# A hybrid attention, SSD and mixture-of-experts layer: VectorE's work of the attention stage in another order, Silu of z later, and ended groups' values copied out of PSUM by ScalarE

## The reference

```python
s = einsum(q, k_cmp) - slopes * dist;  p_cmp = masked_softmax(s);  o_cmp = p_cmp @ v_cmp   # 63 compressed keys
imp = p_cmp @ ov;  idx = top_k(score(imp), 8)                                              # blocks of 64 keys
o_slc = softmax over the chosen blocks @ v_sel                                             # up to (c+1)*128 keys
o_win = softmax over the last 256 keys @ v_win                                             # up to 384 keys
o = gate0 * o_cmp + gate1 * o_slc + gate2 * o_win
# SSD: chunks of 128 tokens; y = (C B^T * decay) X + C state * decay; the output is y * silu(z)
```

## Time and profile before

| | us |
|---|---|
| median of three runs | 1086.52 |
| lowest, highest | 1084.16, 1087.3 |
| the profiled execution | 1083.51 |
| its span | 1081.8 |
| TensorE busy | 1017.3 (94%) |
| VectorE busy | 645.0 (60%) |
| ScalarE busy | 323.3 (30%) |
| GpSimd busy | 175.2 (16%) |

### The profile page before, as it was taken

How to read it: one execution, slowest core, us unless ns; L and a number is a source line. 1 busy time by engine, 2 the same in 40 slices (tenths; PEclk the granted TensorE clock), 3 DMA queues, 4 the chain that set the end, 5 groups by cost and what they waited for, 6 DMA issues and landing times.

```text
span 1081.8 us, 14029 instructions
## 1 busy us (share of the span) xinstructions
PE 1017.3 (94%) x4628; PEld 609.3 (56%) x4629; DVE 645.0 (60%) x1629; ACT 323.3 (30%) x766; POOL 175.2 (16%) x214
## 2 busy tenths in 40 slices
PE   5999999999999899999999899999949999999995
PEld 3444475444556677777788785555524444444442
DVE  2431121555354678666632798765578787878883
ACT  3321121112133566555656564232211000000000
POOL 0020051111000400000000400211021333333432
PEclk9999999999999899999999899999969999999998
DMA  7311042013000200000000503323649879998331
GB/s 256 100 32 40 1 81 78 1 39 101 1 1 1 79 2 1 1 1 1 2 1 1 195 2 103 126 86 110 233 151 374 286 243 333 373 367 308 126 107 70
DMA packets 73686, 119.21 MB, mean 110 GB/s; under 512 B 14016, under 2 KB 53152, under 8 KB 73632
## 3 DMA queue, kind: packets, MB, share of 16 engines
q1 hardware_dynamic: 62544, 87.55, 23.9%
q0 software_dynamic: 11088, 30.95, 8.1%
HBM read 105.37 MB, written 21.50 MB: 117 GB/s over the span
## 4 chain that ended last, share of the span: by engine, by line
PE 52%; DVE 14%; issue 2%; ACT 2%; POOL 0%; DVEq 0%; POOLq 0%; ACTq 0%
PE ps L1763 16%; PE ps L1116 8%; PE ps L1773 8%; PE ps L2086 5%; PE ps L1084 4%; PE ps L1095 4%; DVE ring_gate_up L1246 2%; PE ps L2096 2%; PE ps L1137 2%; DVE misc L285 2%; PE ps L2117 1%; DVE big_u L2302 1%; ACT big_u L1192 1%; DVE ring_down L2424 1%; DVE big_u L1533 1%
## 5 line engine op out<-in xcount | busy, mean ns | idle before, releaser
L1577 DVE STREAM_TRANSPOSE big_w<-big_w 32x256 f32<-32x256 f32 x384 | 167.3, 436 | 30.6 <-DMA big_w<-hn_dram,misc 24.4
L1763 PE MATMUL ps<-ring_gate_up,big_w 128*128 (+1 forms) x400 | 180.6, 595 | 0.0
L498 PE MATMUL ps<-big_w,big_u 128*128 128x512 f32 (+1 forms) x448 | 173.4, 542 | 0.0
L498 PEld LDWEIGHTS ps<-big_w,big_u 128*128 128x128 f32 x448 | 83.8, 191 | 76.0 <-issue 69.3
L1116 PEld LDWEIGHTS ps<-ring_down,big_u 128*128 128x128 f32 x912 | 112.3, 196 | 23.6 <-issue 12.1
L1116 PE MATMUL ps<-ring_down,big_u 128*128 128x65 f32 x912 | 118.6, 277 | 7.3 <-DVEq L1271 3.7
L1763 PEld LDWEIGHTS ps<-ring_gate_up,big_w 128*128 128x128 f32 x400 | 74.5, 192 | 83.8 <-issue 83.8
L1246 DVE CUSTOM_DVE_ANT_0 ring_gate_up<-ps,ring_down 128x384 f32<-128x384 f32 (+7 forms) x128 | 73.8, 629 | 64.8 <-PE ps L1084 63.7
L1192 ACT ACTIVATE big_u<-ps 128x512 f32<-128x512 f32 (+1 forms) x126 | 69.5, 582 | 125.1 <-PE ps L1095 125.0
L1184 ACT ACTIVATE ring_gate_up<-ring_gate_up,big_w 128x64 f32<-128x64 f32 (+8 forms) x192 | 92.2, 555 | 1.1 <-DVE big_w L1246 1.1
L1773 PE MATMUL ps<-ring_down,big_w 128*128 x200 | 90.0, 593 | 0.6 <-ACT big_w L1807 0.6
(11 more groups left out here) (384 smaller groups left out, 1325.4 us busy)
## 6 DMA issues: line engine op xcount, KB each, us to landing
ring_gate_up<-in_w_gate SPq DMA_DIRECT2D x16, 1024.0 KB, 10.0
ring_gate_up<-in_w_up SPq DMA_DIRECT2D x16, 1024.0 KB, 12.7
ring_down<-in_w_down SPq DMA_DIRECT2D x16, 1024.0 KB, 14.8
misc<-in_x SPq DMA_DIRECT2D x16, 512.0 KB, 3.4
big_w<-in_w_in SPq DMA_DIRECT2D x6, 1024.0 KB, 7.7
big_w<-in_w_out SPq DMA_DIRECT2D x8, 512.0 KB, 4.9
hn_dram<-big_u SPq DMA_DIRECT2D x8, 512.0 KB, 2.6
out<-ring_gate_up SPq DMA_DIRECT2D x8, 512.0 KB, 3.8
```

Source lines behind the costliest of these rows:

```text
L498: last = nc.tensor.matmul(ps[:, b, 0:width], uT[:, k, c * P:(c + 1) * P], wbuf[:, n % 2, k, 0:width], start=(k == 0), stop=(k == KD - 1))
L1577: last = nc.vector.transpose(dst[j * 32:(j + 1) * 32, :, i * 32:(i + 1) * 32], src[i * 32:(i + 1) * 32, :, j * 32:(j + 1) * 32])
L1763: last = nc.tensor.matmul(ps[:, 2 + b, :], xT[:, b, k, :], ring_gu[:, bass.ds(at + k * 2 * D_EXP, BANK)], start=(k == 0), stop=(k == KD - 1))
```

## The change

1. ScalarE gets `copy_values(gi)`: one Copy of both value banks (128 x 520 float32, 648 for CMP) into SBUF (`o_copy`), for each group but the last, after `exponentials(j)` of iteration j = last slot + 2. `o_read` now counts these copies; VectorE's reads of the copy are counted by `o_used`, for which the next copy waits.
2. `read_values` reads `o_copy` (for the last group still PSUM) and waits for the copy.
3. In VectorE's iteration, `read_values` stands ahead of `select` and `queries`, and the quarters of the queries start at the CMP slot of a chunk, not at its WIN slot.
4. z's pieces fill six slots, not seven, and the wait for the copies stands ahead of the second pair of slot 7's scores.
5. Silu of z and the table load move behind the decay exponentials of SSD chunk 0; VectorE's product with z waits for it at chunk 3 (`z_ready`).
6. `chunk_in(0)` (now a function of its own, called by `first_vector`, its operations the same) runs on VectorE ahead of the last `read_values`. TensorE's state product of chunk 0 waits for the attention rows (`rows_done`).
7. `weightsT` takes other places in the same buffer, so that the SSD operands of chunk 0 don't lie on it.

```diff
@@ -943,7 +943,8 @@
     q_rows = M["q_rows"]
     scores_full, max_ready, exp_done = sem("scores_full"), sem("maxima_ready"), sem("exp_done")
     wT_full, wT_done = sem("weights_transposed"), sem("weightsT_copied")
-    pv_done, o_read = sem("slot_values_done"), sem("values_read")
+    pv_done, o_read, o_used = sem("slot_values_done"), sem("values_copied"), sem("copied_values_used")
+    o_copy = M["misc"][:, 2048:2048 + NG * GQ * (HD + 17)].rearrange("p (g n) -> p g n", g=NG)
     sel_ready, sel_full, sel_rows = sem("selection_ready"), sem("selection_transposed"), sem("selection_rows")
...
@@ -999,7 +1000,8 @@
 
     def weightsT(j, k):
 
-        return uT[:, 4 * ((J - 1 - j) % 2) + k, 0:BANK]
+        at = ((4096, 6144, 4608, 6656) if (J - 1 - j) % 2 == 0 else (0, 1024, 2048, 3072))[k]
+        return M["big_u"][:, at:at + BANK]
 
     heads_before, copies_before = [0], [0]
...
@@ -1024,19 +1026,19 @@
 
     queries_at = {0: [(1, 0), (1, 1)], 1: [(1, 2), (1, 3)]}
     for c in range(1, NT - 1):
-        j0, n = first_slot[WIN, c], first_slot[CMP, c + 1] - first_slot[WIN, c]
+        j0, n = first_slot[CMP, c], first_slot[CMP, c + 1] - first_slot[CMP, c]
         for quarter in range(4):
             queries_at.setdefault(j0 + quarter * n // 4, []).append((c + 1, quarter))
 
     first_wide = first_slot[WIN, 2]
     n_pieces = (NT - Z_HEAD) * KD
     piece_at, done = {}, 0
-    for j in range(first_wide):
-        n = n_pieces * (j + 1) // first_wide - done
+    for j in range(first_wide - 1):
+        n = n_pieces * (j + 1) // (first_wide - 1) - done
         piece_at[j], done = (done, done + (n + 1) // 2, done + n), done + n
     z_copy_at = {}
     for c in range(Z_HEAD, NT):
-        z_copy_at.setdefault(next(j for j in range(first_wide) if piece_at[j][2] >= (c - Z_HEAD + 1) * KD), []).append(c)
+        z_copy_at.setdefault(next(j for j in piece_at if piece_at[j][2] >= (c - Z_HEAD + 1) * KD), []).append(c)
     z_bank = lambda c: 2 + c % 2
 
...
@@ -1065,11 +1067,11 @@
                     pe.wait_ge(sel_rows, sel_count[c])
             if j >= 1:
                 pe.wait_ge(max_ready, heads_before[j])
-            if j == first_wide:
-                pe.wait_ge(z_copied, NT - Z_HEAD)
             n = columns(j)
             chosen = br == SEL and c in sel_count
             for i, r in enumerate(pairs):
+                if j == first_wide and i == 1:
+                    pe.wait_ge(z_copied, NT - Z_HEAD)
                 for at in range(0, n, BANK):
                     w = min(BANK, n - at)
                     if chosen:
...
@@ -1191,11 +1193,21 @@
                 w = len(blocks) * P
                 nc.scalar.activation(weightsT(j, k)[:, 0:w], ps[:, 4 + copy_use[use] % 2, 0:w], ACT.Copy).then_inc(wT_done, 1)
 
+        def copy_values(gi):
+            br, c = groups[gi]
+            act.wait_ge(pv_done, last_slot[br, c] + 1)
+            if gi >= 1:
+                act.wait_ge(o_used, gi)
+            n = GQ * (HD + 17 if br == CMP else HD + 1)
+            nc.scalar.activation(o_copy[:, :, 0:n], ps[:, 6:8, 0:n], ACT.Copy).then_inc(o_read, 1)
+
         for j in range(J + 1):
             if j >= 1:
                 copy_weights(j - 1)
             if j < J:
                 exponentials(j)
+            if j >= 2 and slots[j - 2][0] != slots[j - 1][0]:
+                copy_values(slots[j - 2][0])
             for c in z_copy_at.get(j, ()):
                 act.wait_ge(z_full, c - Z_HEAD + 1)
                 nc.scalar.activation(z[:, c, :], ps[:, z_bank(c), :], ACT.Copy).then_inc(z_copied, 1)
@@ -1205,10 +1217,6 @@
                 o.mark(nc.scalar.activation(head_rows[:, 1, :], head_rows[:, 1, :], ACT.Exp))
                 o.done(nc.scalar.activation(flat(0), flat(6), ACT.Exp, scale=-1.0))
                 nc.scalar.activation(flat(0), flat(0), ACT.Ln, bias=1.0).then_inc(dt_sem, 1)
-        act.wait_ge(z_copied, NT - Z_HEAD)
-        zs = z[:, Z_HEAD - 1:NT, :]
-        nc.scalar.activation(zs, zs, ACT.Silu)
-        nc.scalar.preload_act_table_set("natural_log_exp_and_others")
 
     def vector(dve):
...
@@ -1250,9 +1258,14 @@
         def read_values(gi):
 
             br, c = groups[gi]
-            dve.wait_ge(pv_done, last_slot[br, c] + 1)
             w = HD + 17 if br == CMP else HD + 1
-            O = ps[:, 6:8, 0:GQ * w].rearrange("p g (r n) -> p g r n", r=GQ)
+            if gi < len(groups) - 1:
+                dve.wait_ge(o_read, gi + 1)
+                O = o_copy[:, :, 0:GQ * w]
+            else:
+                dve.wait_ge(pv_done, last_slot[br, c] + 1)
+                O = ps[:, 6:8, 0:GQ * w]
+            O = O.rearrange("p g (r n) -> p g r n", r=GQ)
             dst, tmp = by_head(o_att[:, c, :]), by_head(M["o_tmp"])
             gate_at = {CMP: 0, SEL: 1, WIN: 2}[br]
...
@@ -1268,10 +1281,10 @@
                     o.mark(nc.vector.tensor_tensor(imp_h.rearrange("p (g r j) -> p g r j", g=NG, r=GQ), O[:, :, :, HD + 1:w],
                                                    d.unsqueeze(3).broadcast_to([P, NG, GQ, N_BLK]), ALU.mult))
                 o.done(nc.vector.tensor_tensor(dst, O[:, :, :, 0:HD], fb, ALU.mult))
-                dve.sem_inc(o_read, 1)
+                dve.sem_inc(o_used, 1)
             else:
-                nc.vector.tensor_tensor(tmp, O[:, :, :, 0:HD], fb, ALU.mult).then_inc(o_read, 1)
-                dve.wait_ge(o_read, gi + 1)
+                nc.vector.tensor_tensor(tmp, O[:, :, :, 0:HD], fb, ALU.mult).then_inc(o_used, 1)
+                dve.wait_ge(o_used, gi + 1)
                 o.done(nc.vector.tensor_tensor(o_att[:, c, :], o_att[:, c, :], M["o_tmp"], ALU.add))
                 if gi == len(groups) - 1:
                     dve.sem_inc(rows_done, 1)
...
@@ -1321,12 +1334,8 @@
                 scores_with_distance(j)
             if j == 0:
                 gates()
-            if j in select_at:
-                c, steps = select_at[j]
-                for step in steps:
-                    select(c, step)
-            for c, quarter in queries_at.get(j, ()):
-                queries(c, quarter)
+            if j == J + 1:
+                next_vector(dve)
             if j >= 2 and (j == J + 1 or slots[j - 2][0] != slots[j - 1][0]):
                 gi, br, c, pairs = slots[j - 2]
                 read_values(gi)
...
+                for step in steps:
+                    select(c, step)
+            for c, quarter in queries_at.get(j, ()):
+                queries(c, quarter)
             if j in sel_at:
                 selection_to_rows(sel_at[j])
...
@@ -1456,6 +1471,8 @@
                 last = nc.tensor.matmul(ps[:, YD_BANK, h * HD:(h + 1) * HD], mT[:, c % 2, h, :], x_dt[:, c % 2, h, :],
                                         start=True, stop=True)
             last.then_inc(y_full, 1)
+            if c == 0:
+                pe.wait_ge(AT.rows_done, 1)
             if c + 1 < NT:
                 for g in range(NG):
...
@@ -1492,6 +1509,10 @@
             if c >= 2:
                 square(c - 2)
             if c == 0:
+                act.wait_ge(AT.z_copied, AT.z_tiles)
+                zs = z[:, Z_HEAD - 1:NT, :]
+                nc.scalar.activation(zs, zs, ACT.Silu).then_inc(z_ready, 1)
+                nc.scalar.preload_act_table_set("natural_log_exp_and_others")
                 act.wait_ge(AT.rows_done, 1)
...
@@ -1554,20 +1579,19 @@
                                         ALU.add).then_inc(st_ready, 1)
             if c >= 1:
                 o.done(nc.vector.tensor_tensor(yb, yb, x_skip[:, b], ALU.add))
+            if c == Z_HEAD - 1:
+                dve.wait_ge(z_ready, 1)
             nc.vector.tensor_tensor(o_ssm[:, c, :].rearrange("p (h d) -> p h d", h=SH), yb,
                                     z[:, c, :].rearrange("p (h d) -> p h d", h=SH), ALU.mult).then_inc(y_ready, 1)
 
-        dve.wait_ge(prep_done, 3)
-        dve.wait_ge(set_up, 1)
-        chunk_in(0)
         for c in range(NT):
             if c + 1 < NT:
-                chunk_in(c + 1)
+                chunk_in(dve, o, c + 1)
             else:
                 next_transposes()
             chunk_out(c)
 
-    return Parts(sync, gpsimd, tensor, scalar, vector), ready, lambda pe: operands(pe, 0)
+    return Parts(sync, gpsimd, tensor, scalar, vector), ready, lambda pe: operands(pe, 0), first_vector
 
 
...
```

More of the change, by code:

```diff
@@ L915, in score_slots, with attend @@
     return [[0, 1], [2, 3]] if n <= 4 else [[0], [1], [2], [3]]
-def attend(nc, N, M, A, C, out, next_tensor):
+def attend(nc, N, M, A, C, out, next_tensor, next_vector):
     sem = N.sem
@@ L1349, in vector @@
                                             ALU.mult).then_inc(dt_sem, 1)
+            if j in select_at:
+                c, steps = select_at[j]
+                for step in steps:
+                    select(c, step)
+            for c, quarter in queries_at.get(j, ()):
+                queries(c, quarter)
             if j in sel_at:
@@ L1392, in ssd @@
```

(55 more changed lines are left out.)

## The result

The changed kernel takes 1135.76 us (median, 1129.89 to 1138.49) against 1086.39 us before: a ratio of 1.045, 95% interval 1.040 to 1.050. The profiled execution took 1138.49 us, its span is 1136.7 against 1081.8. The forecast was 1104.3 with a range to 1115: the right direction, and less than half of the loss. The profiled execution is the slowest of the four (54.9 us above the profile before, where the medians differ by 49.4); what follows is read from the profiles.

A forecast was written before the change was run, and what follows sets the result against it. TensorE was taken to bound the attention stage. Terms 8.0 + 6.8 + 1.8 + 2.3 + 7.0 - 2.5 - 4.4 - 1.2 = +17.8 us on 1083.5 gave 1101.3, plus 3.0 for the median: 1104.3, range 1084 to 1115.

The forecast's parts named there:

- What bounds the kernel: In the attention stage, TensorE's order of work sets the time; each microsecond it waits there is one of the kernel.
- The hand-overs: At ends of value groups, TensorE waits for ScalarE's copy queued behind exponentials: 8.0, 6.8, 1.8 and 2.3, in sum 18.9 us.
- SEL to CMP: Five hand-overs from a selected to a compressed group (SEL 1 to 5): copy 1.85 to 2.0 us late, +8.0 net.
- CMP to WIN: Six hand-overs from a compressed to a window group, chunks 2 to 7: a longer wait for ScalarE, +6.8 us.
- VectorE's new order: Reading first delays selection and maxima, so TensorE's scores wait in chunks 4 to 7: +7.0 us, the least sure term.
- I count nothing: After selected-to-compressed hand-overs, VectorE's read, query quarter and maxima (5.15 us) add nothing beyond the wait already counted.
- z's term: At z's copy early in attention, a wait and half clock go, SEL 0's copy gives back 2.2: -2.5 us.
- rival 2: The hand-overs cost but are partly absorbed by existing waits: +1.4 to +9 us, 1088 to 1095; chance 0.14.
- The clock: TensorE's clock in attention: one fall, at 463 us, goes (-1.2 us); no falls counted at the new waits.
- Rival 3: TensorE's clock falls at the new waits, four or more times: +5 to +13 us more, 1109 to 1117; chance 0.15.
- The end of attention: From attention into the first SSD chunks, TensorE goes on without a gap and Silu comes later: -4.4 us.
- Rival 1: VectorE's waits go and nothing takes their place: 19.4 us faster, 1067.1, or 1080 if half holds; chance 0.13.

The follow-up runs named there:

- e9: The changed kernel with ScalarE's copies at only five of the 23 hand-overs (SEL 1 to SEL 5), VectorE reading PSUM at the others: 1098.0 us.
- e1: The changed kernel without ScalarE's copies; VectorE reads ended groups from PSUM in its new place, all else kept: 1071.5 us.
- e3: The changed kernel with VectorE's order as before (selection and queries ahead of the read), copies and all else kept: 1113.0 us.
- e7: The kernel before the change with only z's part added (pieces in six slots, earlier wait): 1079.8 us.
- e2: The kernel before the change with only ScalarE's copies added; VectorE's order, z, Silu and first SSD chunk as before: 1118.7 us.
- e4: The changed kernel with all 23 copies moved earlier in ScalarE's queue, ahead of the exponentials: 1091.9 us.
- e6: The changed kernel without the copies and with VectorE's order as before; the z, Silu and first SSD chunk parts kept: 1076.1 us.
- e5: The changed kernel with ten useless 128x128 transposes put on TensorE ahead of each of 17 waits: 1119.7 us.

## Why the prediction was wrong, point by point

**What bounds the kernel: right.** TensorE sets the stage, and its delays weren't taken in elsewhere. e9 is the test: five waits of 8.3 us in sum raised TensorE's idle time by 12.2 us against e1; had delays been taken in, it would have risen by less than 8.3.

**The hand-overs: right in sum, and in place at SEL to CMP.** SEL to CMP was put at 1.85 to 2.0 us gross and +1.6 net, and the waits for the copy there are 1.64 to 1.70. The copies took 0.59 and 0.70 us, as estimated from the 0.58 of the 512 columns. CMP to WIN was put at +6.8 for chunks 2 to 7; there TensorE waited 2.23 us for the copy of chunk 2 and 0.57 us for the other five together. At each of these five it had been held up just ahead, behind the copy of the SEL group before, at the maxima or the selection (below). So the waits for the copy, given as some 20 with 25 to 30 us, came to 17 with 21.1.

**VectorE's new order: right for the selection in chunks 5 to 7, and waits in places that it hadn't named.** The forecast had 1.6 + 2.7 + 1.8 = 6.1 for chunks 5, 6 and 7; the waits for the maxima there are 3.0, 2.7 and 1.8, 7.4 in all. The 0.9 for chunk 4 isn't there. After SEL to CMP the forecast says "I count nothing"; there TensorE waited 2.42 us (behind the copy of SEL 1) and 1.47 us (SEL 2) for the maxima, and 1.66 us behind the copy of WIN 1, the 5.5 of the view above. What VectorE does in that time is what the forecast had added up to 5.15 us: the read, a query quarter and the maxima. At SEL 1:

```profile
401.23 1.25 DVE L285 STREAM_TRANSPOSE misc<-ring_gate_up 32x128 f32<-32x128 f32 x4
...
404.55 2.93 PE L1086 MATMUL ps<-ring_down,misc 64*128 64x384 f32 x8 [2.42 <-DVE big_w L1254]
```

And a step was missing. `selection_to_rows` stands at the end of VectorE's iteration, and TensorE's transposes wait for the PSUM bank that it frees. The read ahead of it now waits for the copy, and a query quarter comes in between. At the end of SEL 3 (with VectorE's SSD constants from line 1353 on in the same place):

```profile
475.94 0.20 DVE L1276 RECIPROCAL big_w<-misc 128x8 f32<-128x8 f32 x1 [5.92 <-ACT misc L1202]
...
478.58 1.25 DVE L285 STREAM_TRANSPOSE misc<-ring_gate_up 32x128 f32<-32x128 f32 x4
479.84 0.29 DVE L1318 TENSOR_SCALAR big_w<-ps 128x128 bf16<-128x128 f32 x1
...
480.19 1.97 PE L1097 MATMUL ps<-ident,ring_gate_up 128*128 128x128 f32 x8 [2.52 <-DVE big_w L1318]
```

That is 4.8 us in three places, 2.2 with the old order (e3).

**All waits together: right.** Idle time rose by 25.2 us. The forecast's steps, without the clock and the end, sum to 18.9 (hand-overs) + 7.0 - 2.5, of which 3.3 was the clock's share of z: 18.9 + 7.0 + 0.8 = 26.7, 1.5 more. (z's term is added up wrongly: -2.0 - 3.3 + 2.2 is -3.1 and not -2.5. So is rival 2's upper end, which is 17.8 - 7.0 = 10.8 and not 9. Neither changes the outcome.) The agreement isn't only one of the sum. From the column "idle": z's part alone took 3.1 us away (15.9 to 12.8; forecast 2.0), the copies under the old order added 19.7 (12.7 to 32.4; forecast 18.9, and 2.2 for SEL 0 in z's term), the new order on top of them 8.6 (32.4 to 41.0; forecast 7.0).

**The clock: the step that failed.** The forecast said "I take none", and even counted -1.2 and -3.3 for falls that would go, 4.5 together. Measured: +31.9. It reasoned from a single wait: one of 1.04 us had no fall behind it, and a few falls were kept for a rival, at +5 to +13. There were 12, with 85.3 us in sum. Add 31.9 + 4.5 = 36.4 to the forecast's +17.8, less 1.5 for the waits, plus 2.4 for the end (below), and the sum is 55.1; the span grew by 54.9. Rival 3 named the mechanism, with a chance of 0.15, and priced it at no more than a third of its size. The trace before held a warning: each of the two longest waits of the stage (3.20 and 1.77 us) had a fall behind it, and so had the one of 3.49 us just behind the stage (half clock from 597.8 to 604.6), though one of 1.60 had none. The forecast itself expected some fifteen waits of 1.4 to 2.4 us; nothing for the clock was the most favourable value, not a middle one.

**z: right by itself, lost in company.** e7 gives -6.4 us in the median for -5.3 forecast (2.0 + 3.3). In the changed kernel the wait for z is gone too, but at 358.12 stands a wait of 1.63 us for the copy, and the clock is at half from 359.2 to 369.5.

**The end of attention: right, then half hidden.** TensorE starts chunk 1's operands 0.11 us after the start of its last matmul of values and not 3.76. In e1 the stage from there to chunk 7's operands takes 44.5 us against 48.9: the 4.4 of the forecast (to the tenth, which is luck). ScalarE, which set that number, in e1:

```profile
585.78 1.28 ACT L1498 ACT_TABLE_LOAD   x1
587.08 2.34 ACT L1498 ACTIVATE ring_gate_up<-ring_gate_up 128x2560 f32<-128x2560 f32 x1
589.43 1.28 ACT L1499 ACT_TABLE_LOAD   x1
590.73 0.63 ACT L1503 ACTIVATE misc<-ring_down 128x512 f32<-128x512 f32 x1
```

The table loads cost 1.28 us each, with 0.02 us to the activation behind them. The 2.66 us for a switch that the Trainium skill gives ("ScalarE: Activation LUTs", "What ACT_TABLE_LOAD costs") would by the forecast's estimate have left 1.6 us of the gain; the measurement decides against it here. In the changed kernel only 2.0 us of it show. There the clock was at half once more, from 663.0 to 666.4; at 0.42 to 0.52 us lost for each (last section) that is 1.4 to 1.8 of the missing 2.4, and the rest stays open.

The rule of the Trainium skill that spoke for the change ("VectorE: DVE Perf Modes", "Rules for kernel authors": copy PSUM to SBUF first for many operations) found nothing to save: the 128x512 multiply in float32 takes 0.69 us from the copy, as it did from PSUM.

```profile
575.06 0.69 DVE L1286 TENSOR_TENSOR big_w<-misc,big_w 128x512 f32<-128x512 f32 x1
```

**Rival 1** (nothing takes the waits' place) is e1 in all but name: what would have been had the copies not been there, with -15 us in place of the -19.4 that was priced.

## What to carry to other kernels

An engine that is idle four tenths of the time, as ScalarE was in this stage, isn't free at the moment you need it: when a step moves to another engine, look up what stands ahead of it in that engine's list, and compare that end, not the step's duration, with the time at which the consumer is ready. When such waits come on TensorE again and again (here 4 to 26 us apart), price half clock behind them too: here it cost more (31.9 us) than the waits (25.2 us). A reordering that reads early gains only as long as what it reads comes early; switch both parts apart before you judge either.

## What the runs showed of the hardware that was not expected

Between kernels, attention minus TensorE's idle time and minus the 272.0 us of e1 leaves the cost of the half clock: 36.7 us for 85.3 at half (after), 15.9 for 30.7 (e2), 21.9 for 44.4 (e3), 12.9 for 30.7 (e9), 5.1 for 10.2 (e4). So a microsecond at half clock cost 0.42 to 0.52 us.

What TensorE did before its clock fell: in the changed kernel it waited 1.5 to 3.0 us again and again, 4 to 26 us apart, the longest 2.97. The length of a single wait doesn't tell whether a fall follows; the same wait went both ways. VectorE's second SSD chunk held TensorE up for 2.35 us in e1 and in the changed kernel:

```profile
595.56 0.41 PE L1421 MATMUL ps<-ident,ring_gate_up 128*128 128x128 f32 x2 [2.35 <-DVE big_u L1534]
```

```profile
662.03 0.41 PE L1437 MATMUL ps<-ident,ring_gate_up 128*128 128x128 f32 x2 [2.35 <-DVE big_u L1550]
```

The first (e1) had no fall behind it, the second had one from 663.0 to 666.4. The stage's first wait for a copy, 1.70 us, had a fall behind it in the changed kernel (at 335.3) and in e3, and none in e2. In e4 one of 2.56 us (at 359.0) had none, in e6 and e7 one of 1.37 us had 6.8 us of half clock behind it (at 427), though the last wait of over 1 us ahead of that was 38 us away. In sum the waits did matter: matmuls of no use in 1.3 us ahead of 17 of them (e5) brought 85.3 us down to 10.2. What exactly the chip counts stays open.
